# Three-block transformer kernel on one core: other SBUF places for the activation tiles

## What is computed

```
h = rms_norm(x, norm_mix[l])
x = x + pool_attn_mixer(h, ...)          # l = 0; l = 1: rglru_mixer
h = rms_norm(x, norm_ffn[l])
x = x + conv_ffn(h, ...)                 # u, g = split(causal_dwconv(h @ w_in)); (gelu(g) * u) @ w_out
...
x = x + mixers(h @ w_in) @ w_o           # second model
x = x + relu(h @ ffn_w1)^2 @ ffn_w2
```

## Time and profile before

| quantity | value |
|---|---|
| median of three runs | 1110.89 us |
| profiled execution, its span | 1112.8 us |
| TensorE busy | 1070.7 us, 96% |
| weight loads busy | 1016.0 us, 91% |
| VectorE busy | 838.8 us, 75% |
| ScalarE busy | 631.2 us, 57% |
| mean DMA rate | 180 GB/s |
| mean granted TensorE clock | 0.986 |

### The profile page before, as it was taken

How to read it: one execution, slowest core, us unless ns; L and a number is a source line. 1 busy time by engine, 2 the same in 40 slices (tenths; PEclk the granted TensorE clock), 3 DMA queues, 4 the chain that set the end, 5 groups by cost and what they waited for, 6 DMA issues and landing times.

```text
span 1112.8 us, 20978 instructions
## 1 busy us (share of the span) xinstructions
PE 1070.7 (96%) x8608; PEld 1016.0 (91%) x8608; DVE 838.8 (75%) x1433; ACT 631.2 (57%) x1059; POOL 66.0 (6%) x79
## 2 busy tenths in 40 slices
PE   8999999999999899999999997999999999999996
PEld 7877899999988798999999897899989989999996
DVE  6467998887797968987787779998965687755452
ACT  7546676655666847665565693322333368875340
POOL 1231100000002001000000000000000020000010
PEclk9999999999999989999999999999999999999998
DMA  9368455566666855767766542232334365566651
GB/s 366 120 210 291 143 199 186 187 175 191 190 217 225 305 167 171 245 222 238 239 209 193 179 156 90 72 96 92 123 107 145 105 229 174 189 190 188 185 158 38
DMA packets 59424, 200.41 MB, mean 180 GB/s; under 512 B 6720, under 2 KB 10432, under 8 KB 59200
## 3 DMA queue, kind: packets, MB, share of 16 engines
q1 hardware_dynamic: 57600, 194.54, 54.4%
q10 hardware_dynamic: 1728, 4.53, 1.1%
HBM read 197.99 MB, written 1.05 MB: 179 GB/s over the span
## 4 chain that ended last, share of the span: by engine, by line
PE 81%; DVE 11%; ACT 4%; DMA 2%; issue 1%; ACTq 0%; POOL 0%; SPq 0%; DVEq 0%
PE ps L480 81%; DVE wlo L1575 3%; ACT whi L1050 1%; ACT L1050 1%; DVE rst L1608 1%; ACT hh L1050 1%; DVE hl L1581 1%; DMA ring<-pa_w_out 1%; DMA ring<-rg_w_out 1%; DVE x L1575 1%; DMA ring<-pa_w_in 0%; DMA ring<-w_o 0%; DVE raw L1575 0%; DVE w L1575 0%; DVE bks L1575 0%
## 5 line engine op out<-in xcount | busy, mean ns | idle before, releaser
L480 PE MATMUL ps<-hh,whi 128*128 128x256 f32 (+1 forms) x1656 | 475.4, 287 | 4.3 <-DVE hl L1575 2.8
L480 PE MATMUL ps<-hl,whi 128*128 128x256 f32 (+1 forms) x1656 | 465.9, 281 | 0.0
L480 PE MATMUL ps<-hh,wlo 128*128 128x256 f32 (+1 forms) x1656 | 465.1, 281 | 0.0
L1575 DVE TENSOR_TENSOR wlo<-ring,whi 128x1024 fp32r<-128x1024 f32 (+2 forms) x314 | 376.1, 1213 | 58.5 <-ACT whi L1050 57.9
L1050 ACT ACTIVATE whi<-ring 128x1024 fp32r<-128x1024 f32 (+2 forms) x314 | 322.3, 1037 | 73.9 <-PE ps L480 56.0
L480 PEld LDWEIGHTS ps<-hh,whi 128*128 128x128 f32 x1656 | 314.3, 190 | 25.3 <-issue 14.6
L480 PEld LDWEIGHTS ps<-hl,whi 128*128 128x128 f32 x1656 | 314.4, 190 | 1.3 <-issue 1.0
L480 PEld LDWEIGHTS ps<-hh,wlo 128*128 128x128 f32 x1656 | 314.3, 190 | 0.0
L480 PE MATMUL ps<-hidl,whi 128*128 128x256 f32 x608 | 170.5, 280 | 0.0
L480 PE MATMUL ps<-hidh,wlo 128*128 128x256 f32 x608 | 170.3, 280 | 0.0
L480 PE MATMUL ps<-hidh,whi 128*128 128x256 f32 x608 | 170.3, 280 | 0.0
(11 more groups left out here) (364 smaller groups left out, 1331.6 us busy)
## 6 DMA issues: line engine op xcount, KB each, us to landing
ring<-ffn_w_in SPq DMA_DIRECT2D x88, 512.0 KB, 3.6
ring<-ffn_w SPq DMA_DIRECT2D x64, 512.0 KB, 3.8
ring<-w_in SPq DMA_DIRECT2D x51, 512.0 KB, 3.4
ring<-ada_w SPq DMA_DIRECT2D x48, 512.0 KB, 4.1
ring<-ffn_w_out SPq DMA_DIRECT2D x32, 448.0 KB, 3.4
ring<-rg_w_in SPq DMA_DIRECT2D x20, 512.0 KB, 4.4
ring<-ffn_w_out SPq DMA_DIRECT2D x16, 512.0 KB, 3.6
ring<-pa_w_in SPq DMA_DIRECT2D x15, 512.0 KB, 7.0
```

What stands on the lines that cost most here:

```text
L480: return e.matmul(o, l, r, start=start, stop=stop)
L1575: return e.tensor_tensor(o, a, b, op)
```

## The change

Only sizes of tiles change: rows of `hh` and `hl` are 64 floats longer, and the unused tiles have other sizes. The instructions of all five engines are the same, in the same order and with the same waits; only addresses differ.

```
-        hh = alloc(ctx, "hh", [128, 8, T + 64], F32R)
-        hl = alloc(ctx, "hl", [128, 8, T + 64], F32R)
+        hh = alloc(ctx, "hh", [128, 8, T + 128], F32R)
+        hl = alloc(ctx, "hl", [128, 8, T + 128], F32R)
...
-        alloc(ctx, "fill", [128, 56])       # ahead of whi and the ring
+        alloc(ctx, "fill", [128, 96])
...
-        alloc(st, "fill", [128, 48])        # ahead of pah, pal
+        alloc(st, "fill", [128, 8])
...
-        alloc(st, "fill", [128, 8])         # ahead of the first hidh, hidl
+        alloc(st, "fill", [128, 120])
...
-        alloc(st, "fill", [128, 56])        # ahead of yh, yl
+        alloc(st, "fill", [128, 88])
...
-        alloc(st, "fill", [128, 16])        # ahead of the second hidh, hidl
+        alloc(st, "fill", [128, 104])
...
-        alloc(s2, "fill", [128, 16])        # ahead of mgh, mgl
+        alloc(s2, "fill", [128, 56])
...
-        alloc(st, "fill", [128, 48])        # ahead of hid2h, hid2l
+        alloc(st, "fill", [128, 128])
```

## The result

The changed kernel is slower: median 1124.47 us of five runs (1117.72 to 1125.79) against 1110.26 us of five (1107.17 to 1111.19) before. The ratio is 1.0109, 95% interval 1.0081 to 1.0138. The forecast was 1088 us, 1074 to 1113, faster with a chance of 0.65. It was wrong, and on the other side.

What follows compares the result with a forecast made beforehand. The prediction took TensorE's matmul pitch to bound the kernel. Its terms, 17.3 + 4.8 + 1.7 + 0.5 - 0.8 = 23.5 us, came off the 1110.89 us median to give 1087.4, forecast as 1088 us, range 1074 to 1113.

Steps and rivals of the forecast that it cites:

- What bounds the kernel: Whole kernel: TensorE, busy 96% of 1112.8 us, so the start-to-start pitch of one matmul is the price.
- That the place sets the pitch: Matmuls of `pa` at distance 192 take 113.3 ns, other families about 117.8, because of their place.
- the pitch at 128: `hh` and `hl`, 4968 matmuls: from 117.2 to 113.3 ns, saving 3.9 ns each, together 17.3 us.
- Wrong altogether: Sign that the forecast fails: `hid` at distances 224 and 160 still at 117.8 ns.
- The upper bound of 119: `hh` and `hl` at distance 128: at worst 119 ns a matmul, a little above the costly 117.8.
- Rival 1: No change: place isn't what makes `pa` cheap, or the cheap zone misses 128; 1109 to 1111 us; chance 0.18.
- the two `hid`: First `hid` to distance 224, second to 160: 1056 matmuls from 117.8 to 113.3 ns, 4.8 us saved.
- the alternation: `hh` rows alternating between distances 288 and 32 settle at 116.7 ns, where constant costly distances have 117.8.
- Rival 2: Slower: `hh` loses its useful alternation and 128 is costly; 1114.4 us at 117.8 ns, 1119.7 at 119; chance 0.16.
- the share that reaches the end: `hh` and `hl` savings count in full in the three feed-forward stages (2880 matmuls), three quarters elsewhere (2088).
- Rival 3: Deeper trough: 128 lies near a 110 ns floor, `hh` saves 7.2 ns a matmul; 1071 us; chance 0.09.
- Addresses on the other engines at nothing: VectorE, ScalarE and GpSimd at other addresses: taken as 0, with 2.4 us either way kept in the range.

Runs made afterwards that it cites:

- s4_hh128: The kernel before with only `hh` and `hl` changed, to constant distance 128; 1118.19 us, ratio 1.0083.
- s2_all192: The kernel before with all seven tile families placed at distance 192 from the weights, weights at 384 modulo 512; 1094.97 us, ratio 0.9872.
- u3_all192b: `s2_all192` run again unchanged; 1095.77 us, ratio 0.9866.
- r2_lows: `s2_all192` with only low tiles moved (first `hid` 128 bytes further, second 64, `hid2` 32, also `y` and `pa`), weights unmoved; 1106.77 us.
- p1_pair: `s2_all192` with `wlo` and every low tile 128 bytes further; 1136.65 us.
- u2_wlo128: `s2_all192` with `wlo` 128 bytes further and nothing else moved; 1092.65 us, ratio 0.9836 to the kernel before.
- r3_wlo: `s2_all192` with `wlo` 128 bytes further and a few low tiles moved (second `hid` 64, `hid2` 128, `y` 192); 1103.65 us.

## Why the prediction was wrong

**What bounds the kernel: right.** The only change of a busy time that matters is TensorE's 7.6 us.

**That the place sets the pitch: right.** The same three matmuls per row have 113 to 121 ns by places alone. The rule that the prediction quoted from the Trainium skill ("TensorE: Matmul & The Clock Gate", Part 2: loads of the next weights take no read bandwidth from the running matmul) would have them all equal. The runs disagree with that consequence. They do not show whether reads collide or something else does it.

**The step that failed: the pitch at 128.** The prediction said "Of these I take 113.3, since 128 is nearest to the measured 192". It measured 118.7 to 120.0 ns. The cost as a function of distance is not smooth: 192 has 113.3 and 200 has 120.0. Nearness says nothing, and the same step failed for 160 (117.3 to 117.5 against 113.3), 224 (118.3 to 118.5) and 256 (120.0 against 115.5). By the prediction's own signs this is "Wrong altogether". The upper bound of 119 was also too low by 1 ns. Evidence against the step was there: `hh` alternated between 288 and 32, and `hid` lay at 288, 320 and 448, so four remainders modulo 512 had nearly one pitch and one had another. That speaks for an isolated place rather than for a zone. Rival 1 named it (a zone so narrow that 128 misses it), but still let the two `hid` gain 4.8 us in it; they gained nothing.

**The second failure: one reading per place was taken as the place's price.** `hid2` at 448 was "costly" in one execution and cheap in another. The trace before hinted at it: `hh` had 117.7 ns in one feed-forward and 116.7 in the other at the same distances. The prediction put that down to the alternation. It may also explain a part of the time: an execution before in which `hid2` draws the cheap pitch is 768 x 4.3 = 3.3 us faster than one in which it draws the dear one, and the profiled one, which drew the dear one, lay 4.3 us above the median. Then the change cost `hid2` more in most executions than the traces say. With one trace of the kernel before, this is an estimate and not shown.

**Rival 2 named the side and priced it too low.** Its 1114.4 to 1119.7 us used 117.8 and 119 ns. With the measured pitches: in the three feed-forwards `hh` rose from 117.2 to about 119.5, so 2880 x 2.3 = 6.6 us; elsewhere 2088 x 2.3 x 0.75 = 3.6 us. `hid2` adds 768 x 2.2 = 1.7, `pa` 192 x 3.4 = 0.7, the first `hid` 0.3, less 0.2 for the second. That is 12.7 us of the 14.2, of which `hh` alone is 10.2. This fits the share that reaches the end, but does not test it: `s4_hh128` measured 8.8 with `hh` at 118.7 ns only and with a cheap `hid2`, so draws of some us stand in every such comparison. The chance of 0.16 for this side turned out too small.

**Rival 3, a floor near 110 ns:** no stretch of any placement ran below 113.2 ns.

**Addresses on the other engines at nothing: right as far as busy time shows it.** VectorE is busy 838.9 us against 838.8.

**All families at 113.3 ns** had been estimated at some 25 us; the drawn 117.8 and the stages with waits left about 14 (`s2_all192`, `u3_all192b`).

**Open:** what in the chip makes places differ, why two pitches are stable, what a break decides by, and why moving `wlo` alone removes the dear one.

## What to carry to other kernels

In this kernel, where TensorE is busy 96% of the time with a weight load beside every matmul, the SBUF place of the one operand against the other was worth 1 to 2% of the time. In a kernel like it, measure the start-to-start pitch in a gap-free stretch at each candidate place, in more than one execution, and do not interpolate between places: 8 bytes away may be another case. A profile's span is one draw; compare pitches stretch by stretch and times by medians.

## What the runs showed of the hardware

- The pitch of fp32r matmuls of 256 columns, each with a load of 128 columns of weights, at full granted clock depends on the distance of moving rows and weights: 113.3 or 117.8 ns at 192 and 448; 117.8, rarely 113.3, at 64; 116.7 or 117.8 at 32 and 288; 117.4 at 160; 118.3 at 224; 118.7 to 120.0 at 128; 120.0 at 200 and 256; 119.1 at 176 and 208.
- Moving everything together by 352 bytes leaves it as it was. A shift of one family by 256 bytes gives the same two pitches, 113.3 and 117.8 ns.
- At 192 the same program has stretches of 60 us and more at 113.3 ns in one execution and at 117.8 in the next. That the draw makes a part of the 3 to 8 us between runs of one kernel is likely, not shown.
- From 113.3 ns at 192, moving the low tile by 32 to 128 bytes against the high one costs 4 to 6 ns a matmul (`r2_lows`); moving it and `wlo` by 128 costs 7.6 (`p1_pair`). Moving `wlo` alone by 128 leaves 113.3 and all but removes 117.8 (3 of 1417 groups of `hh` in `u2_wlo128`, 2 of 1415 in `r3_wlo`).
